# Queries and latent keys that come out of their products already turned, in a two-layer hybrid attention trunk

## What is computed

```
for l in range(2):
    proj = (rms(x) * g) @ w_in            # q_a 16x64 | k_a 2x64 | v_a 2x64 | c_q 384 | c_kv 256 + k_pe 32 | two gates of 1024
    A: rope(q_a), rope(k_a); window of 2 chunks of 64; softmax with a sink per head; y_a
    B: q_b = rms(c_q) @ w_uq              # 8 heads x (64 plain + 32 rotated)
       k_b = rms(c_kv) @ w_ukv -> 64 plain columns a head, and v_b 64 a head; k_pe rotated, one for all heads
       dense softmax, causal by chunks of 64; y_b
    x = x + rms((sigmoid(gate_a) * (y_a @ w_oa) + sigmoid(gate_b) * (y_b @ w_ob)) @ w_out)
    x = x + rms(relu(rms(x) @ w_mlp_in)**2 @ w_mlp_out)
```

## Time and profile before

| | |
|---|---|
| median of 3 runs | 763.9 us |
| the profiled execution's own time | 763.82 us |
| its span | 762.1 us |
| TensorE busy | 98% of the span, granted clock 0.998 |
| VectorE, ScalarE, GpSimd busy | 67%, 55%, 22% |
| DMA | 132.16 MB, 173 GB/s over the span |
| chain that ended last | TensorE 90%, VectorE 6%, ScalarE 2% |

### The profile page before, as it was taken

How to read it: one execution, slowest core, us unless ns; L and a number is a source line. 1 busy time by engine, 2 the same in 40 slices (tenths; PEclk the granted TensorE clock), 3 DMA queues, 4 the chain that set the end, 5 groups by cost and what they waited for, 6 DMA issues and landing times.

```text
span 762.1 us, 10863 instructions
## 1 busy us (share of the span) xinstructions
PE 747.8 (98%) x3970; PEld 631.5 (83%) x3970; DVE 512.4 (67%) x674; ACT 417.0 (55%) x789; POOL 164.7 (22%) x250
## 2 busy tenths in 40 slices
PE   6999999999999999999999999999999999999996
PEld 5978887888798888888888888788888988888885
DVE  5789867667765666656686887685568656565664
ACT  6847675534564444444577676654348444544452
POOL 1966422100131111100125443220002210111110
PEclk9999999999999999999999999999999999999999
DMA  7739533455465555566337493335463656564521
GB/s 256 254 99 299 186 111 111 151 182 171 158 201 186 193 193 171 163 216 207 104 103 257 174 304 111 111 111 168 164 220 111 221 166 221 176 209 171 202 68 55
DMA packets 68619, 132.16 MB, mean 173 GB/s; under 512 B 2874, under 2 KB 10596, under 8 KB 68324
## 3 DMA queue, kind: packets, MB, share of 16 engines
q1 hardware_dynamic: 68308, 131.64, 52.1%
q10 hardware_dynamic: 272, 0.00, 0.0%
HBM read 130.59 MB, written 1.05 MB: 173 GB/s over the span
## 4 chain that ended last, share of the span: by engine, by line
PE 90%; DVE 6%; ACT 2%; issue 1%; DMA 1%; POOL 0%; SPq 0%; POOLq 0%; ACTq 0%; DVEq 0%
PE acc L1353 18%; PE acc L1355 17%; PE acc L1354 17%; PE tp L1640 6%; PE sc L1640 6%; PE tp L1328 4%; PE sc L1435 3%; PE acc L1387 3%; PE tp L1642 3%; PE sc L1642 3%; DVE w_lo L995 2%; PE sc L1353 1%; PE sc L1354 1%; PE sc L1355 1%; DVE x L1160 1%; PE sc L1626 1%
## 5 line engine op out<-in xcount | busy, mean ns | idle before, releaser
L995 DVE TENSOR_TENSOR w_lo<-raw,w_hi 128x1024 fp32r<-128x1024 f32 (+3 forms) x256 | 307.9, 1222 | 163.0 <-ACT w_hi L654 161.4
L654 ACT CAST w_hi<-raw 128x1024 fp32r<-128x1024 f32 (+3 forms) x256 | 251.3, 996 | 181.1 <-PE acc L1355 107.9
L1353 PE MATMUL acc<-w_hi,s_hi 128*128 128x512 f32 (+1 forms) x328 | 127.7, 389 | 0.0
L1355 PE MATMUL acc<-w_hi,s_lo 128*128 128x512 f32 (+1 forms) x328 | 126.6, 386 | 0.0
L1354 PE MATMUL acc<-w_lo,s_hi 128*128 128x512 f32 (+1 forms) x328 | 126.5, 386 | 0.0
L1353 PE MATMUL acc<-w_hi,s_both 128*128 128x512 f32 (+2 forms) x320 | 122.0, 381 | 1.0 <-DVE w_lo L995 0.6
L1355 PE MATMUL acc<-w_hi,s_both 128*128 128x512 f32 (+2 forms) x320 | 118.5, 370 | 0.0
L1354 PE MATMUL acc<-w_lo,s_both 128*128 128x512 f32 (+2 forms) x320 | 118.4, 370 | 0.0
L517 POOL TENSOR_TENSOR tok<-k_b 128x512 f32<-128x512 f32 x32 | 36.9, 1159 | 266.0 <-ACT k_b L750 244.7
L1353 PEld LDWEIGHTS acc<-w_hi,s_hi 128*128 128x128 f32 x328 | 61.6, 188 | 13.1 <-DVE w_lo L995 1.3
L1355 PEld LDWEIGHTS acc<-w_hi,s_lo 128*128 128x128 f32 x328 | 61.6, 188 | 12.3
(11 more groups left out here) (186 smaller groups left out, 1076.0 us busy)
## 6 DMA issues: line engine op xcount, KB each, us to landing
raw<-in_w_mlp_in SPq DMA_DIRECT2D x32, 1024.0 KB, 5.4
raw<-in_w_mlp_out SPq DMA_DIRECT2D x32, 1024.0 KB, 5.0
raw<-in_w_in SPq DMA_DIRECT2D x24, 1024.0 KB, 5.4
raw<-in_w_oa SPq DMA_DIRECT2D x8, 1024.0 KB, 5.0
raw<-in_w_out SPq DMA_DIRECT2D x8, 1024.0 KB, 4.9
raw<-in_w_ob SPq DMA_DIRECT2D x4, 1024.0 KB, 5.0
raw<-in_w_in SPq DMA_DIRECT2D x3, 768.0 KB, 4.8
raw<-in_w_in SPq DMA_DIRECT2D x4, 576.0 KB, 6.5
```

The costliest lines, as they stand in the source:

```text
L654: s.copy(split_view(w_hi, p), raw_view(p)).then_inc(hi_ready, 1)
L995: v.tensor_tensor(split_view(w_lo, p), raw_view(p), split_view(w_hi, p).bitcast(F32), ALU.subtract)\
L1353: mm(banks[t][:, 0:N], h[:, kk, tk], wh[:, k, :], start=(start and k == 0), stop=False)
L1355: ins = mm(banks[t][:, 0:N], low[:, kk, tk], wh[:, k, :], start=False, stop=(stop and k == b - a - 1))
```

## The change

- q of kind A is made with the weights standing still and 256 tokens moving (`turned_product`), in `acc[2:4]` and in `sc`, so head dimensions are in the rows. GpSimd makes rows of cosines and sines times 1/rms of x, TensorE turns them (`angles`), ScalarE copies them (`turned_cs`), and VectorE multiplies each bank by them in four operations (`multiply_q`), straight from the bank to `qT_a`. The rotated query is not summed: `qT_a` holds cosine part and sine part in 128 rows, and `kT_a` holds the rotated key and its swapped, partly negated copy, so that the score matmul adds them.
- GpSimd scales the latents by 1/rms ahead of their turn (`latent_scaled`); before, ScalarE scaled the products.
- `w_uq` comes as two loads by column kind: `uqp` (32 rotated columns of each head) and `uqn` (64 plain ones), each in three DMAs, ahead of the second half of q. `uqp` is multiplied with tokens in the rows, rotated by GpSimd and turned in one turn (`qpe`); `uqn` and the key half of `w_ukv` come out turned (`turned_piece`), the value half with tokens in the rows (`token_piece`). ScalarE copies them from the banks (`nope_copy`). k_pe is turned once (`kpe`), and GpSimd copies it to the other heads.
- `MIDDLE` and `END` are gone. Two memsets of GpSimd (`qT_a`, `kT_a`, lines 564 and 565) are gone.

```diff
-    + [("q", 4, COL)] * 4 + [("uq", KQ, BQL)] * 2 + [("ukv", KV, COL)] * 2
+    + [("q", 4, COL)] * 2 + [("uqp", KQ, BH * BR)] + [("uqn", KQ, COL)] + [("q", 4, COL)] * 2 + [("ukv", KV, COL)] * 2
...
-MIDDLE = {0: [("qA", 1, 0)], 1: [("qA", 1, 1)], 2: [("kB", 0, 0)], 3: [("qB", 1, 0)], 4: [("kB", 1, 1)]}
-END = {1: [("qB", 0, 0)], 2: [("qB", 0, 1), ("kB", 0, 1)], 3: [("kB", 1, 0), ("qB", 1, 1)]}
-FIRST_USE = {3: [("qA", 1, 0)], 5: [("qA", 1, 1)], 7: [("qB", 0, 0), ("kB", 0, 0)], 8: [("qB", 0, 1), ("kB", 0, 1)],
-             9: [("qB", 1, 0), ("kB", 1, 0)], 11: [("qB", 1, 1), ("kB", 1, 1)]}
...
+                    if n == 8:
+                        heads = w_uq[l].rearrange("(k p) (h d) -> p k h d", p=P, h=BH)
+                        for d0, d1 in ((BN, BQK), (0, BN)):
+                            raw_free(pos, n)
+                            for k in range(KQ):
+                                sp.dma_start(raw[:, n % RAW, k * BH * (d1 - d0):(k + 1) * BH * (d1 - d0)]
+                                             .rearrange("p (h d) -> p h d", h=BH),
+                                             heads[:, k, :, d0:d1]).then_inc(raw_full[n % RAW], 16)
+                            n += 1
...
+                for name, c0, N in (("cq", 0, BQL), ("ckv", BQL, BKL)):
+                    for t in range(TT):
+                        to_rstd(pos, (name, t))
+                    for t in range(TT):
+                        c = SUMS[(name, t)]
+                        pool.wait_ge(rstd_ready, pos.count(NSUM, c + 1))
+                        rows = latent[:, t, c0:c0 + N]
+                        g.tensor_tensor(rows, rows, rstd[:, c:c + 1].to_broadcast([P, N]), ALU.mult).then_inc(latent_scaled, 1)
...
+                pool.wait_ge(rstd_ready, pos.count(NSUM, TT))
+                for t in range(TT):
+                    scale = rstd[:, SUMS[("x", t)]:SUMS[("x", t)] + 1].unsqueeze(2).to_broadcast([P, 4, AD // 2])
+                    for a, table in enumerate((cost[:, t, :], sint[:, t, 1, :])):
+                        ins = g.tensor_tensor(scaled_cs[:, a, t], table.unsqueeze(1).to_broadcast([P, 4, AD // 2]), scale,
+                                              ALU.mult)
+                ins.then_inc(angle_rows, 1)
...
+                    halves = k_a[:, t, :, :].rearrange("p h (u c d) -> p h u c d", u=2, c=2)
+                    steps.link(pool_rope(halves[:, :, 0], AKV, AD // 2, t, 1))
+                    g.tensor_copy(halves[:, :, 1, 0], halves[:, :, 0, 1])
+                    g.tensor_scalar(halves[:, :, 1, 1], halves[:, :, 0, 0], -1.0, None, ALU.mult).then_inc(pool_roped, 1)
...
+            def nope_copy(dst, h0, src):
+
+                for odd in range(2):
+                    ins = s.copy(dst[0:BN, h0 + odd:h0 + 4:2, :],
+                                 src[odd * BN:(odd + 1) * BN, :].rearrange("p (h n) -> p h n", h=2))
+                ins.then_inc(proj_out, 1)
...
+                hi(pos, 18)
+                turned_copy(pos, ("angles",))
+                turned_hi(pos, ("ckv",))
+                hi(pos, 20)
+                used(pos, 17)
+                for t in range(TT):
+                    s.copy(gate_b[:, t, 0:BH * BR], sc[0][:, t * BH * BR:(t + 1) * BH * BR]).then_inc(proj_out, 1)
+                hi(pos, 22)
+                used(pos, 19)
+                for u in range(2):
+                    nope_copy(qT_b, 4 * u, acc[u])
+                turned_copy(pos, ("kA",))
+                turned_copy(pos, ("kpe",))
...
+            def multiply_q(pos, c, u):
+
+
+                src = (acc[2:4], sc)[c][u][:, :].rearrange("p (x c q) -> p x c q", x=2, c=NCHUNK)
+                for odd in range(2):
+                    rows = slice(odd * AD, (odd + 1) * AD)
+                    for a in range(2):
+                        to = slice((a + odd) % 2 * AD, ((a + odd) % 2 + 1) * AD)
+                        table = turned_cs[rows, a].rearrange("p (c q) -> p c q", c=NCHUNK).unsqueeze(1)\
+                            .to_broadcast([AD, 2, NCHUNK, CHUNK])
+                        ins = v.tensor_tensor(qT_a[to, c, :, odd, u].rearrange("p c (x q) -> p x c q", x=2), src[rows], table,
+                                              ALU.mult)
+                ins.then_inc(q_multiplied, 1)
...
-                dve.wait_ge(tables_ready, 1)
-                for c, p in ((0, 18), (1, 22)):
-                    lo(pos, p)
-                    dve.wait_ge(proj_out, pos.count(14, 2 * PROJ[f"q{c}"] + 1))
-                    rope(v, steps, probs[:, 0, :], q_of_group(0, c).rearrange("p h (c d) -> p h c d", c=2), AG, AD // 2, 0, 1,
-                         between=lambda: lo(pos, p + 1)).then_inc(roped, 1)
-                    dve.wait_ge(roped, pos.count(2, c + 1))
-                lo(pos, 25)
-                turned(pos, ("qA", 0, 0))
-                lo(pos, 27)
-                turned(pos, ("qA", 0, 1))
+                dve.wait_ge(bank_done(("angles",)), bank_turn(pos, ("angles",)))
+                lo(pos, 18)
+                used(pos, 15)
+                multiply_q(pos, 0, 0)
+                lo(pos, 20)
+                multiply_q(pos, 0, 1)
+                lo(pos, 26)
+                used(pos, 23)
+                multiply_q(pos, 1, 0)
+                lo(pos, 28)
+                multiply_q(pos, 1, 1)
...
+            def turned_product(pos, p, banks, free=None, between=None):
+
+                for i in range(4):
+                    if i == 2 and between is not None:
+                        between()
+                    pe.wait_ge(lo_ready, pos.count(NP, 2 * RAW + p + i + 1, 8))
+                    wh, wl = (split_view(w, p + i).rearrange("p (k n) -> p k n", k=2) for w in (w_hi, w_lo))
+                    for f in range(4):
+                        if i == 0 and f % 2 == 0 and free is not None:
+                            free(f // 2)
+                        out, cols = banks[f // 2][:, (f % 2) * SEQ:(f % 2 + 1) * SEQ], slice(f * P, (f + 1) * P)
+                        for k in range(2):
+                            kk = 2 * i + k
+                            mm(out, wh[:, k, cols], s1_hi[:, kk, :], start=(i == 0 and k == 0 and f % 2 == 0), stop=False)
+                            mm(out, wh[:, k, cols], s1_lo[:, kk, :], start=False, stop=False)
+                            ins = mm(out, wl[:, k, cols], s1_hi[:, kk, :], start=False, stop=(i == 3 and k == 1 and f % 2 == 1))
+                    ins.then_inc(piece_used, 1)
...
+                turned_product(pos, 12, pair[1], free=latent_free(1))
+                pe.wait_ge(angle_rows, pos.count(1, 1))
+                turn(pos, ("angles",), [scaled_cs[:, a, t].rearrange("p r i -> p (r i)") for a in range(2) for t in range(TT)])
+                pe.wait_ge(latent_scaled, pos.count(2 * TT, 2 * TT))
                 turn(pos, ("ckv",), [latent[:, t, BQL + k * P:BQL + (k + 1) * P] for t in range(TT) for k in range(KV)])
-                for i, p in enumerate(range(16, 20)):
-                    product(pos, p, 4 * (i // 2), s1, pair[0], i == 0, i == 3, free=projected(pos, "kv") if i == 0 else None)
+                for p in (16, 17):
+                    token_piece(pos, p, s2, 0, sc[0], lambda w, k: w[:, k, :], p == 16, p == 17)
+                for p in (18, 19):
+                    turned_piece(pos, p, s2, 0, pair[0], lambda w, k, f: w[:, k, f * P:(f + 1) * P], p == 18, p == 19,
+                                 free=projected(pos, "kv"))
+                pe.wait_ge(pool_roped, pos.count(6, 2 * POOL_ROPED["kpe"] + 2))
+                turn(pos, ("kA",), [k_a[:, t, g, :] for g in range(AKV) for t in range(TT)])
+                turn(pos, ("kpe",), [latent[:, t, BQL + BKL:BQL + BKL + BR] for t in range(TT)])
+                pe.wait_ge(proj_out, pos.count(10, 2 * PROJ["uqp"] + 2))
+                turned_product(pos, 20, sc)
+                pe.wait_ge(pool_roped, pos.count(6, 2 * POOL_ROPED["qB"] + 2))
+                turn(pos, ("qpe",), [gate_b[:, t, b * P:(b + 1) * P] for b in range(2) for t in range(TT)])
...
-                for c, (q, before, k0) in enumerate((("uq0", "q0", 0), ("uq1", "q1", 0), ("ukv0", "uq0", KQ), ("ukv1", "uq1", KQ))):
-                    if c == 0:
-
-                        pe.wait_ge(pool_roped, pos.count(8, 2 * POOL_ROPED["kA"] + 2))
-                        for t in range(TT):
-                            turn(pos, ("kA", t), [k_a[:, t, :]])
-                    elif c < 3:
-
-                        pe.wait_ge(roped, pos.count(2, c))
-                        extra(pos, ("qA", 0, c - 1))
-                    for i in range(2):
-                        product(pos, 20 + 2 * c + i, k0, s2, pair[1 - c % 2], i == 0, i == 1,
-                                free=projected(pos, before) if i == 0 else None)
-                for t in range(TT):
-                    turned(pos, ("kA", t))
-                for g in range(AKV):
-                    turned(pos, ("qA", 0, g))
```

(62 more changed lines are left out.)

218 lines of the change are left out of this document (74 added, 144 removed).

## The result

The changed kernel takes 765.35 us (median of 12 runs, 764.73 to 766.18) where the kernel before took 764.06 us in the same comparison: a ratio of 1.0017, 95% interval 1.0009 to 1.0025. The forecast was 760.4 us and faster. It is 0.17% slower, inside the 0.2% that was named as no change. The profiled execution took 764.95 us for a span of 763.0 us, 0.9 us more than the span of the kernel before. One of the 12 runs of the kernel before took 1066.0 us, and single runs of later comparisons 1236.5 and 1872.6 us; the medians hardly move with them.

What follows compares the result with a forecast made beforehand. TensorE's own stream was taken to bound the kernel: +1.44 +0.47 (projections) -8.4 (rounds) +1.35 +1.7 (new wait) = -3.4 us, from a profiled 763.82 us to 760.4 us. Range 757.2 to 764.8 us.

Steps and rivals of the forecast that it cites:

- Projections, +1.44 and +0.47: From c_q's turn to the first scores: TensorE's stream grows 1.44 us in layer 1, 0.47 in layer 0.
- Rounds, -4.2 a layer: First scores to last turn of probabilities: without MIDDLE and END turns, TensorE's stream shortens 4.2 us a layer, 8.4 in two.
- The new wait, 1.35 and 1.7: Behind the first half of q: TensorE awaits piece 19's low part behind four multiplications, 1.35 us layer 1, 1.7 layer 0.
- The second four "just in time": VectorE's second four multiplications, between low parts of pieces 20 and 21, are covered by a 2.9 us product piece.
- GpSimd, nothing: Rstd, scaling of c_q and key rotation on GpSimd finish before they are wanted, covered by w_in products; cost nothing.
- GpSimd late: Rival: c_q's scaling in layer 0 or rotated keys come late, 1 to 3 us, 761.4 to 763.4 us; chance 0.08.
- Loads, nothing: Loads uqp and uqn, 11.5 us for both at 30 ns a packet, land before they are needed; cost nothing.
- rivals on packets: Small packets make loads late: 40 to 48 ns, 764.5 us, chance 0.13; above 48 ns, 772 or 855, chance 0.12.

## Why the prediction was wrong

- *Projections, +1.44 and +0.47*: right. Without waits the stretch is 37.89 and 37.86 us for 37.78 forecast.
- *Rounds, -4.2 a layer*: the stream is right (63.27 for 63.4). The step that failed is "a round that is 0.9 to 1.4 us shorter still covers what the probabilities need", and with it the cost of nothing. It counted what work the rounds lose and not where the work that stays stands. The copy of `qpe` is one turn's copy in place of several, but all of it is in round 0, directly ahead of the high part that the row maximum waits for through VectorE's queue. Moving it gave back 1.33 us a layer. About 0.28 us a layer stay, with a cause that is open between the shorter round and the copies in their new place; without them the stream is about 63.0 us, 0.4 less than forecast.
- *The new wait, 1.35 and 1.7*: right in place, releaser and mechanism. Both stretches between the turn of c_kv and kA's turn are 1.45 us longer than their matmuls. The four multiplications took 2.80 us where 2.75 was expected. In layer 0 `neg_sink` was not slower (0.34 us for two in both layers).
- *The second four "just in time"*: wrong, 0.80 us a layer. From the moment that piece 19 is ready, VectorE needs 1.7 us (low part of 20), 2.8 (block) and 1.2 (low part of 21), 5.7 together; TensorE is there after 1.5 us (rest of piece 19), 0.6 (turns) and 2.9 (piece 20), 5.0. Only a piece of 2.9 us was set against the block of 2.8, and the two low parts were left out.
- *GpSimd, nothing*: the scalings were ready in time (31.1 us for 30.8), so the rival "GpSimd late" did not happen. What failed is the other side of the same contention: the price beside a busy neighbour was weighed for GpSimd and not for VectorE. 0.60 us in layer 0. The Trainium skill, "GPSIMD Engine Reference", Specifications, says that GpSimd's interface to SBUF is shared with VectorE and contends with instructions of VectorE that have two SBUF inputs. A low part is one, and the trace agrees: 1.30 us beside the scaling, 0.69 without it.
- *Loads, nothing*: right, though the price of a packet, 30 ns, was about twice the 13 and 19 ns of the rows, and none of the rivals on packets came true. By the Trainium skill, "DMA: Bandwidth & Descriptors", Specifications, transfers under 512 bytes are read, modified and written. No run here shows the reading back itself, but the size agrees: the prediction's estimate by it was 5.8 us for both loads (6.1 if twice their 1.18 MB is put over the 0.77 MB in 2 us of the earlier trace rows), and the rows give 6.1 us. The Trainium skill's floor of 10.5 ns a packet (the same page, Bandwidth), taken as one packet at a time over all engines, would give an estimate of about 64 us. The rows show a thousand packets in a microsecond.

The terms add up: 0.10 + 0.80 + 0.11 in layer 1, -0.25 + 0.80 + 0.08 + 0.60 in layer 0, and twice 1.15 in the rounds are 4.5 us between forecast and trace. 4.3 us is the distance of the spans. The three unpriced waits went by edits of the order alone, without undoing the change: the one in the rounds but for about 0.28 us a layer, the one for piece 21 together with the one for piece 19, and the one in layer 0.

## What to carry to other kernels

When a change shortens the stream of the bounding engine, walk each other engine's queue again through the shortened stretch, as a sum of durations from its last wait on: a work item counts where it stands, not how many there are. A block that is not urgent belongs behind enough of the urgent ones to cover it (two here); pushing it back by one may only make the next late. A change that ends level may hold a gain: here 7.5 us were three reorderings away.
